# A one-core hybrid mixer with two attention layers: memory weights rounded on another engine, and E's gate, the dilated attention and even q rearranged

## The chip, the core and the metric

The kernel runs on one core of one Trainium2 chip. The metric is the device time of one execution in microseconds; three runs of the kernel before are given. TensorE (PE; its weight loads are PEld), VectorE (DVE), ScalarE (ACT) and GpSimd (POOL) each run their own program in order; SyncE (SP) issues the weight loads.

## The reference

x is 1024 tokens by 1024 channels, the memory 256 tokens by 1024. A first block has five branches of width 512, each gated and merged; a second block has an even layer (dilated attention, pool, memory attention) and an odd layer.

```python
# first block
h = rms_norm(x);  ys = [y_a, y_b, y_c, y_d, eo * silu(e_z)]     # y_e: attention to k, v of the memory
merged = sum(sigmoid(gates[n]) * (ys[n] @ w_br[n]) for n in range(5))
x = x + rms_norm(merged @ w_out)
# even layer
qk, v_a, x_b, q_m, z = split(rmsnorm(x) @ w_in)
a_out = dilated_attention_mixer(qk, v_a, cos, sin)   # 4 heads; groups (128, 1), (512, 4), (2048, 16)
b_out = multiscale_pool(x_b, w_pool, scale)          # mean over 2, 4, 8, 16 tokens minus x_b, then w_pool
m_out = memory_attention(q_m, mem_n, w_mem_kv)
x = x + (concatenate([a_out, b_out, m_out]) * silu(z)) @ w_out
```

In dilated attention each group yields a numerator, a row maximum and a denominator; the three groups of a head are joined by exp(m_g - max m).

## The kernel before

**Dense products.** Channels lie on the partitions. Every dense product is made as three products of rounded parts (h_hi·w_hi, h_lo·w_hi, h_hi·w_lo; y_hi and y_lo for gated inputs). SP loads a weight tile of 8 (or 4) x 128x128 into one of two slots of w_raw; POOL makes w_hi from it (L3065, four instructions of 128x256) and w_lo (L3070, four), and counts `tiles_split`; TensorE multiplies with 512 tokens at a time (`dense_half`, L344), two PSUM halves in turn. The halves are taken by ScalarE (`project`, L399 and L401; `project_away`, L1237, which sends them to DRAM in L1214; `memory_kv`, L1340), or by VectorE (`merge`, L474 and L476, behind ScalarE's sigmoid L458; `add_out`, L492).

**Order.** `section()` opens a part of the program with three threads, dense, aux and side. `stage(name, us, ahead, ...)` adds to a thread a piece for some of PE, ACT and DVE, with a planned length; each engine's program merges the threads by planned time (`play`, L3010), and runs in that order. Before its part in a stage, an engine waits for what the other engines have done in the stages ahead in the thread, unless it stands in `ahead` (`thread_part`, L2995).

**Memory keys and values.** E's k (`memory_beside`, beside D's x), E's v, and k and v of the even and the odd layer (`memory_kv`) are 24 weight tiles for 256 columns each. Even and odd k v run beside branch A's chunk work (L1622, L1713, L1741 to L1756) and branch B's convolution on VectorE (taps L1532).

**E.** E's attention (L2035, L2051, L1010, L1020) runs beside D's merge; then the E gate (`gate_stored`: per half tile L1285 product with z, L1287 y_hi, L1288 y_lo, all VectorE) and E merge, with the angle work of rope (L2112 to L2133) on VectorE in another thread. Stage "C merged" is a `drain` on TensorE that waits for VectorE's parts ahead of it.

**Dilated attention** (`dilated_attention`, L2376). A head has 18 slots: 6 turn v (L2426), 12 are pairs of blocks. For a pair in slot i: scores on TensorE (L2437, L2438) at i, bias, maximum (L2518, L2525, L2526, VectorE) at i + 0.4, exponentials (L2486, ScalarE) at i + 1, turn (L2447, TensorE) at i + 1.4, copy (L2495, ScalarE) at i + 1.8, mix (L2460, TensorE) at i + 2.2, take (L2532 to L2537, VectorE) at i + 2.5. Buffers of pairs alternate: bias of pair m waits for the turn of pair m - 2. The stages of the next head's projections (L344) fill the time between, with rope (L2352 to L2355) on VectorE. `dilated_join` (L2562 spread on TensorE, L2585 and L2596 ScalarE, L2589 to L2628 VectorE) joins a head. Beside head 3 runs "pool x"; behind it "even q", then the pool sums (L2701 to L2706), "x back", "even out A" (`add_out`, waits for join 3) and pool mix (L2735). The output x is kept in DRAM (`x_fm`) meanwhile.

## Time and profile before

| | us |
|---|---|
| three runs | 3713.05, 3718.22, 3718.74 (median 3718.22) |
| the profiled execution, its span | 3720.16, 3718.3 |
| TensorE busy, its weight loads | 3428.0 (92%), 2787.2 (75%) |
| VectorE busy | 1769.0 (48%) |
| GpSimd busy | 1568.3 (42%) |
| ScalarE busy | 907.8 (24%) |

Busy shares are averages over stages with different limits: TensorE at 92% still idles 290 us, and those are spread over many waits. The mean clock granted to TensorE is 0.966 of full speed; the stretches below 1 lie mostly at waits.

### The profile page before, as it was taken

What the parts mean: (1) busy time and instruction counts of PE and PEld (TensorE: products, weight loads), DVE (VectorE), ACT (ScalarE), POOL (GpSimd) and SP (SyncE); (2) the same over time, 40 slices, a digit from 0 to 9 for tenths busy, and PEclk for the clock granted to TensorE, in tenths of its full rate; (3) what the DMA queues carried; (4) which work ended last, traced back from release to release, by engine and by line L of the source; (5) the groups of instructions that cost most, each with busy time, mean ns of one, the idle gap of its engine ahead of it and who ended that gap; (6) DMA issues with size and microseconds to landing.
All of it is one profiled execution on the core that took longest, in us unless ns stands there. A gap on an engine that the chain in (4) does not pass through costs nothing.

```text
span 3718.3 us, 44394 instructions
## 1 busy us (share of the span) xinstructions
PE 3428.0 (92%) x16512; PEld 2787.2 (75%) x16512; DVE 1769.0 (48%) x2634; ACT 907.8 (24%) x1780; POOL 1568.3 (42%) x2013
## 2 busy tenths in 40 slices
PE   7989989999999999899899899889969989999988
PEld 6778888886786677677677587778757767788767
DVE  4733688774124454533523546675552444412343
ACT  3222212223014432333012322222221122310021
POOL 3454582233452245534444254353314334424423
PEclk9999999999999999999999999999979999999999
DMA  3122121111131021231112111010102101211211
GB/s 116 46 71 60 45 87 26 46 49 47 56 96 41 26 66 34 63 102 40 50 48 91 66 46 29 29 35 22 30 17 88 51 24 46 63 46 37 80 37 68
DMA packets 297208, 196.98 MB, mean 53 GB/s; under 512 B 25365, under 2 KB 277273, under 8 KB 297017
## 3 DMA queue, kind: packets, MB, share of 16 engines
q1 hardware_dynamic: 271241, 132.77, 13.0%
q10 hardware_dynamic: 25776, 61.56, 4.5%
q8 instruction: 132, 2.16, 0.3%
q14 instruction: 59, 0.48, 0.0%
HBM read 168.87 MB, written 25.44 MB: 52 GB/s over the span
## 4 chain that ended last, share of the span: by engine, by line
PE 62%; DVE 11%; PEld 3%; ACT 3%; issue 2%; POOL 2%; DMA 1%; ACTq 0%; PEldq 0%; DVEq 0%; POOLq 0%
PE ps L344 49%; PE ps L982 2%; PEld ps L344 2%; PE ps L1622 2%; POOL w_lo L3070 1%; PEld ps L2562 1%; PE ps L2051 1%; PE ps L995 1%; ACT wrk L1010 1%; POOL w_hi L3065 1%; PE ps L2460 1%; PE ps L1915 1%; PE ps L2447 1%; PE ps L2438 1%; DVE wrk L2604 1%
## 5 line engine op out<-in xcount | busy, mean ns | idle before, releaser
L3065 POOL TENSOR_TENSOR w_hi<-w_raw,pool_one 128x256 fp32r<-128x256 f32 x1004 | 682.0, 708 | 2097.7 <-PE ps L344 2060.6
L344 PE MATMUL ps<-h_hi,w_hi 128*128 128x512 f32 x2928 | 1212.3, 414 | 94.9 <-POOL w_lo L3070 28.2
L344 PE MATMUL ps<-h_hi,w_lo 128*128 128x512 f32 x2928 | 1158.1, 396 | 0.0
L344 PE MATMUL ps<-h_lo,w_hi 128*128 128x512 f32 x2928 | 1157.3, 395 | 0.0
L3070 POOL TENSOR_TENSOR w_lo<-w_raw,w_hi 128x256 fp32r<-128x256 f32 x1004 | 887.3, 913 | 23.1
L344 PEld LDWEIGHTS ps<-h_hi,w_hi 128*128 128x128 f32 x2928 | 560.7, 192 | 265.9 <-issue 104.2
L344 PEld LDWEIGHTS ps<-h_hi,w_lo 128*128 128x128 f32 x2928 | 559.0, 191 | 123.1
L344 PEld LDWEIGHTS ps<-h_lo,w_hi 128*128 128x128 f32 x2928 | 561.9, 192 | 107.6 <-issue 5.5
L344 PE MATMUL ps<-y_hi,w_hi 128*128 128x512 f32 x704 | 287.7, 409 | 15.8 <-issue 11.9
L344 PE MATMUL ps<-y_hi,w_lo 128*128 128x512 f32 x704 | 276.0, 392 | 0.0
L344 PE MATMUL ps<-y_lo,w_hi 128*128 128x512 f32 x704 | 276.0, 392 | 0.0
L1532 DVE SCALAR_TENSOR_TENSOR y_spare<-y_spare_hi,cols,y_spare 128x511 f32<-128x511 f32 (+28 forms) x232 | 200.3, 905 | 2.2 <-DVE y_spare L1532 0.5
L1622 PE MATMUL ps<-wrk 128*128 128x128 f32 x1216 | 162.4, 282 | 18.9 <-DVE wrk L1741 5.0
L474 DVE TENSOR_TENSOR wrk<-ps,wrk 128x512 f32<-128x512 f32 x64 | 44.2, 691 | 279.9 <-PE ps L344 278.8
L1622 PEld LDWEIGHTS ps<-wrk 128*128 128x128 f32 x1216 | 154.7, 196 | 29.5 <-POOL w_lo L3070 10.7
L344 PEld LDWEIGHTS ps<-y_hi,w_hi 128*128 128x128 f32 x704 | 133.3, 189 | 55.9 <-issue 25.5
L458 ACT ACTIVATE wrk<-ps,cols 128x512 f32<-128x512 f32 x80 | 55.2, 689 | 430.6 <-PE ps L344 401.9
L344 PEld LDWEIGHTS ps<-y_lo,w_hi 128*128 128x128 f32 x704 | 133.2, 189 | 29.7 <-issue 3.6
L344 PEld LDWEIGHTS ps<-y_hi,w_lo 128*128 128x128 f32 x704 | 133.1, 189 | 28.6
L492 DVE TENSOR_TENSOR acc<-acc,ps 128x512 f32<-128x512 f32 x72 | 49.5, 687 | 151.3 <-PE ps L344 150.2
L436 DVE TENSOR_TENSOR wrk<-wrk 128x512 f32<-128x512 f32 x48 | 38.5, 803 | 158.1 <-ACT wrk L425 157.9
L1713 ACT ACTIVATE wrk<-ps 128x256 f32<-128x256 f32 x112 | 42.6, 385 | 211.7 <-PE ps L1622 199.1
(399 smaller groups left out, 3950.7 us busy)
## 6 DMA issues: line engine op xcount, KB each, us to landing
w_raw<-in_w_in SPq DMA_DIRECT2D x87, 512.0 KB
w_raw<-in_even_w_in SPq DMA_DIRECT2D x48, 512.0 KB
away<-wrk ACTq DMA_DIRECT2D x64, 256.0 KB, 2.1
w_raw<-in_odd_w_in SPq DMA_DIRECT2D x32, 512.0 KB
wrk<-away ACTq DMA_DIRECT2D x24, 512.0 KB
wrk<-in_x ACTq DMA_DIRECT2D x16, 512.0 KB, 8.0
w_raw<-in_w_br SPq DMA_DIRECT2D x32, 256.0 KB
w_raw<-in_even_w_out SPq DMA_DIRECT2D x24, 256.0 KB
```

The source lines that it names most:

```text
L344: mm = nc.tensor.matmul(ps[:, b, 0:n], w[:, slot, k, :], rhs(part, k, b), start=(k == 0 and q == 0), stop=(k == nk - 1 and q == 2))
L436: ch.link(nc.vector.tensor_tensor(o(j, b), o(j, b), wt(sz, b), ALU.mult))
L458: nc.scalar.activation(wt(gt, b), ps[:, b, :], ACT.Sigmoid, bias=gate_bias(i)).then_inc(dense_free[b], 1)
L474: nc.vector.tensor_tensor(wt(gt, b), ps[:, b, :], wt(gt, b), ALU.mult).then_inc(dense_free[b], 1)
L492: nc.vector.tensor_tensor(y, x, ps[:, b, :], ALU.add).then_inc(dense_free[b], 1)
L982: mm = nc.tensor.matmul(S[:, u, c], l, r, start=True, stop=True)
L995: mm = nc.tensor.transpose(PT[:, kb, u, :], SB[:, u, lo + kb * P:lo + (kb + 1) * P], ident)
L1532: ins = nc.vector.scalar_tensor_tensor(y, x, b_tap(s, i), y, ALU.mult, ALU.add)
L1622: mm = nc.tensor.matmul(four(dst)[:, h, :], lhsT(h), rhs(h), start=True, stop=True)
L1713: nc.scalar.activation(ZZ[:, two, :], four(2 + p)[:, two, :], ACT.Copy).then_inc(gdn_act.sem, 1)
L3065: ins = nc.gpsimd.tensor_tensor(hi, raw, one[:, 0:2], ALU.mult)
L3070: ins = nc.gpsimd.tensor_tensor(lo, raw, hi.bitcast(F32), ALU.subtract)
```

## The change

Five parts. (A) `round_tile`: for the 24 memory tiles ScalarE makes w_hi in one instruction of 128x1024, behind an eviction of its own; POOL then only makes w_lo and waits on `hi_by_act`. (B) Stage "C merged" has TensorE in `ahead`. (C) `gate_stored` for E is replaced by `gate_products` (the products with z, a stage behind E's attention, in the section before) and `gate_parts` (y_hi by ScalarE, y_lo by VectorE). (D) Turn, copy, mix and take of a pair come at i + 2.0, 2.4, 3.0 and 3.4, and a head is planned at 22.0 slots instead of 21.2. (E) Even q goes to DRAM beside head 3 and comes back into acc 4 to 7 after the pool sums; pool x follows it, into acc 4 to 7; even out A stands beside the pool sums in the same section; the lower half of x is loaded behind pool x, the upper one behind join 3.

```diff
         def f_dve(dve):
-            if sum_there:
-                sum_there(dve)
             for j in range(r.n):
                 for b in range(2):
                     yield when(r, j, b)
+                    if sum_there and b == 0:
+                        sum_there(dve, j)
                     out_ready(dve, r.t0 + j, b)
                     x, y = (old or acc_at)(j, b), (new or acc_at)(j, b)
                     nc.vector.tensor_tensor(y, x, ps[:, b, :], ALU.add).then_inc(dense_free[b], 1)
...
+    def gate_products(name, o, z_first, us=8.0):
+
+        gated = sig.take("y_gated", 8)
+
+        def f_dve(dve):
+            for b in range(2):
+                ngates[b] += 1
+                for j in range(4):
+                    yield (4 * b + j) / 8
+                    if j == 0:
+                        dve.wait_ge(gate_loaded[b], 16 * ngates[b])
+                    nc.vector.tensor_tensor(o(j, b), o(j, b), gate_tiles(z_first[b])[:, j, :],
+                                            ALU.mult).then_inc(gated.sem, 1)
+        stage(name, us, dve=f_dve)
+        return gated
+
+    def gate_parts(name, o, gated, before, us=8.0):
+
+        rounded = sig.take("y_rounded", 8)
+        done = sig.take("y_done", 8)
+        part = lambda t, j, b: t[:, j, b * HALF:(b + 1) * HALF]
+
+        def f_act(act):
+            out_ready(act, before.t0 + before.n - 1, 1)
+            for i in range(8):
+                yield i / 9
+                act.wait_ge(gated.sem, gated.nth(i))
+                nc.scalar.activation(part(y_hi, i % 4, i // 4), o(i % 4, i // 4), ACT.Copy).then_inc(rounded.sem, 1)
+
+        def f_dve(dve):
+            out_ready(dve, before.t0 + before.n - 1, 1)
+            for i in range(8):
+                yield (i + 0.9) / 9
+                dve.wait_ge(rounded.sem, rounded.nth(i))
+                nc.vector.tensor_tensor(part(y_lo, i % 4, i // 4), o(i % 4, i // 4),
+                                        part(y_hi, i % 4, i // 4).bitcast(F32), ALU.subtract).then_inc(done.sem, 1)
+        stage(name, us, ("act", "dve"), act=f_act, dve=f_dve)
+        return done
+
...
+    project("A project", r_a, a_tile, lambda j: col("b_aqkv", j), after=lambda act, j: round_tile(act, r_a.t0 + j + 2))
...
-    def memory_kv(name, w_kv, which, kind, place, after_wide):
+    def round_tile(act, t):
+        if t in act_tiles:
+            act.wait_ge(raw_loaded[t % 2], 32 * (t // 2) + 32)
+            act.wait_ge(dense_out, 2 * t - 2)
+            nc.scalar.activation(w_hi[:, t % 2], w_raw[:, t % 2], ACT.Copy).then_inc(hi_by_act, 1)
+
...
+    stage("C merged", 0.1, ("pe",), pe=c_merged_pe)
     on("aux")
...
-    def e_there(dve):
-        dve.wait_ge(e_attended.sem, e_attended.nth(0))
-    stage("E attention there", 0.1, dve=e_there)
-    e_done = gate_stored("E gate", wt, (6, 8))
+    e_done = gate_parts("E gate in parts", wt, e_gated, r_dm)
...
-                events.append((i + 1.4, i, lambda m=m, g=g: turn(m, g)))
-                events.append((i + 2.2, i, lambda m=m, g=g, n=n: mix(m, g, n)))
+                events.append((i + 2.0, i, lambda m=m, g=g: turn(m, g)))
+                events.append((i + 3.0, i, lambda m=m, g=g, n=n: mix(m, g, n)))
             yield from in_time(events)
+            if h == 3:
+                pe.drain().then_inc(last_mixed.sem, 1)
...
-                events.append((i + 1.8, i, lambda m=m, g=g: copy(m, g)))
+                events.append((i + 2.4, i, lambda m=m, g=g: copy(m, g)))
...
-                events.append((i + 2.5, i, lambda m=m, g=g, n=n: take(m, g, n)))
+                events.append((i + 3.4, i, lambda m=m, g=g, n=n: take(m, g, n)))
...
+            at_eq2 = project_away("even q", run(2, *both(w2, C2_Q)), None, None, 1.2, lambda b: wt(9, b))
             r_px = run(2, *both(w2, C2_X))
-            project("pool x", r_px, acc_at, before=lambda act, j, b: head_free(act, 4))
+
+            def x_room(act, j, b):
+                head_free(act, 4)
+                if j == 3:
+                    act.wait_ge(last_mixed.sem, last_mixed.nth(0))
+            project("pool x", r_px, lambda j, b: acc_at(4 + j, b), before=x_room, pace=1.2)
+
+            def x_lower(act):
+                act.dma_start(acc[:, 0:4, :], x_fm.rearrange("k p t -> p k t")[:, 0:4, :]).then_inc(x_lower_in, 16)
+                stored_away(act)
+            stage("lower half of x back", 0.5, act=x_lower)
         on("aux")
         stage("head z before the groups", 11.0)
...
+
+    def first_sum(j, b):
+        return acc_at(j, b) if j < 4 else wt(j, b)
+
+    def x_there(dve, j):
+        dve.wait_ge(x_lower_in if j < 4 else x_upper_in, 16)
+    add_out("even out A", run(4, *both(w2o[0], 0), 4, 4), lambda pe, k, b: pe.wait_ge(join_done.sem, join_done.nth(3)),
+            x_there, first_sum, first_sum)
+    pool_summed = sig.take("pool_summed", 1)
+
+    def pool_sums_there(act):
+        act.wait_ge(pool_summed.sem, pool_summed.nth(0))
+    stage("pool sums there", 0.1, act=pool_sums_there)
     on("aux")
 
     def p_load(act):
+        act.wait_ge(join_done.sem, join_done.nth(3))
+        act.dma_start(wrk[:, 4:8, :], x_fm.rearrange("k p t -> p k t")[:, 4:8, :]).then_inc(x_upper_in, 16)
         load(act, wt(9)[:, 0:HALF].rearrange("p (g d) -> p g d", g=4),
              A["even_w_pool_2"][0].rearrange("g c d -> c g d"))
         yield 0.9
         loads_done(act)
-
-    def x_upper(act):
-        act.wait_ge(join_done.sem, join_done.nth(3))
-        load(act, wrk[:, 4:8, :], x_fm.rearrange("k p t -> p k t")[:, 4:8, :])
-    on("side")
-    stage("last head joined", 22.0)
-    stage("upper half of x back", 0.5, act=x_upper)
-    on("aux")
...
@@ -2704,26 +2784,13 @@
             ch.link(nc.vector.tensor_tensor(small[:, 64:80], src[:, 0:16], C("icount")[:, 16 * i:16 * i + 16], ALU.mult))
             ch.link(nc.vector.scalar_tensor_tensor(wt(i), src, 1.0 / s, x, ALU.mult, ALU.subtract))
             ch.link(nc.vector.tensor_tensor(wt(i)[:, 0:16], small[:, 64:80], x[:, 0:16], ALU.subtract))
-    stage("pool weights", 5.0, act=p_load)
+        dve.drain().then_inc(pool_summed.sem, 1)
+    stage("pool weights, upper half of x back", 5.0, act=p_load)
     stage("pool sums", 26.0, dve=p_dve)
 
...
+    def q_back(act):
+        act.dma_start(acc[:, 4:8, :], away[at_eq2:at_eq2 + 4].rearrange("j p t -> p j t")).then_inc(even_q_in, 16)
+    stage("even q back", 0.5, act=q_back)
...
+
+    def even_q_there(pe):
+        pe.wait_ge(even_q_in, 16)
+    stage("even q there", 0.1, pe=even_q_there)
...
-        def split(t, s, raw_count, nk):
+        def split(t, s, raw_count, nk, by_pool, rounded):
             pool.wait_ge(raw_loaded[s], raw_count)
-            for k in range(0, nk, 2):
+            if rounded is not None:
+                pool.wait_ge(hi_by_act, rounded)
+            for k in range(0, nk, 2) if rounded is None else ():
                 raw, hi, lo = w_raw[:, s, k:k + 2], w_hi[:, s, k:k + 2], w_lo[:, s, k:k + 2]
                 ins = nc.gpsimd.tensor_tensor(hi, raw, one[:, 0:2], ALU.mult)
-            ins.then_inc(hi_ready, 1)
-            pool.wait_ge(hi_ready, t + 2)
+            if rounded is None:
+                ins.then_inc(hi_ready, 1)
+                pool.wait_ge(hi_ready, by_pool)
```

Where the E gate runs, VectorE's queue before (wrk holds E's output and the stored z, ps the PSUM halves):

```order
L2056 COPY wrk<-ps 128x512
L474 TENSOR_TENSOR wrk<-ps,wrk 128x512
L476 TENSOR_TENSOR acc<-acc,wrk 128x512
...
L476 TENSOR_TENSOR acc<-acc,wrk 128x512
L1285 TENSOR_TENSOR wrk<-wrk 128x512
L1287 CAST y_hi<-wrk 128x512
L1288 TENSOR_TENSOR y_lo<-wrk,y_hi 128x512
...
L1288 TENSOR_TENSOR y_lo<-wrk,y_hi 128x512
L2112 CAST wrk<-wrk 32x1024
```

and of the change (L479, L481, L1310, L1333, L2171 are L474, L476, L1285, L1288, L2112 of before):

```order
L2117 COPY wrk<-ps 128x512
L1310 TENSOR_TENSOR wrk<-wrk 128x512 x8
L479 TENSOR_TENSOR wrk<-ps,wrk 128x512
L481 TENSOR_TENSOR acc<-acc,wrk 128x512
...
L481 TENSOR_TENSOR acc<-acc,wrk 128x512
L1333 TENSOR_TENSOR y_lo<-wrk,y_hi 128x512 x8
L479 TENSOR_TENSOR wrk<-ps,wrk 128x512
L481 TENSOR_TENSOR acc<-acc,wrk 128x512
...
L481 TENSOR_TENSOR acc<-acc,wrk 128x512
L2171 CAST wrk<-wrk 32x1024
```

The products with z stand ahead of D's last two gate tiles, y_hi has left the queue, and the first evictions of the E merge stand ahead of the angle work.

In even k v, ScalarE's queue before (L1713 evicts branch A's chunks, L1340 memory tiles):

```order
L1214 DMA away<-wrk 128x512 x2
L1713 ACTIVATE wrk<-ps 128x256 x2
L1340 ACTIVATE wrk<-ps 128x128 x2
L1713 ACTIVATE wrk<-ps 128x256 x2
L1340 ACTIVATE wrk<-ps 128x128 x2
L1713 ACTIVATE wrk<-ps 128x256 x2
L1340 ACTIVATE wrk<-ps 128x128 x2
```

and of the change (L1774, L1394 and L1219 are L1713, L1340 and L1214 of before):

```order
L1774 ACTIVATE wrk<-ps 128x256 x2
L1394 ACTIVATE wrk<-ps 128x128 x2
L1370 ACTIVATE w_hi<-w_raw 128x1024
L1219 DMA away<-wrk 128x512 x2
L1774 ACTIVATE wrk<-ps 128x256 x2
L1394 ACTIVATE wrk<-ps 128x128 x2
L1370 ACTIVATE w_hi<-w_raw 128x1024
L1774 ACTIVATE wrk<-ps 128x256 x2
```

A rounding of 128x1024 stands behind each memory tile's evictions.

From the end of head 3 to the pool mix, ScalarE's queue before (L2585 and L2596: join; L399: pool x, then even q; L1073: loads):

```order
L2495 ACTIVATE wrk<-ps 128x256
L2585 ACTIVATE wrk<-ps 128x1024
...
L2585 ACTIVATE wrk<-ps 128x16x64
L2596 ACTIVATE wrk<-wrk 128x1024 x3
L1073 DMA wrk<-in_even_w_pool 128x4x128
L399 ACTIVATE acc<-ps 128x512 x4
L1073 DMA wrk<-x_fm 128x4x1024
L399 ACTIVATE acc<-ps 128x512
L1073 DMA acc<-x_fm 128x4x1024
L399 ACTIVATE acc<-ps 128x512 x3
L2742 ACTIVATE wrk<-ps,cols 128x512 x8
```

and of the change (L1243 evicts even q, L402 pool x, L2646 and L2657 are the join, L2809 the pool mix):

```order
L1243 ACTIVATE wrk<-ps 128x512
L1219 DMA away<-wrk 128x512
...
L402 ACTIVATE acc<-ps 128x512 x2
L2646 ACTIVATE wrk<-ps 128x1024
...
L2646 ACTIVATE wrk<-ps 128x16x64
L402 ACTIVATE acc<-ps 128x512 x3
L2657 ACTIVATE wrk<-wrk 128x1024 x3
L402 ACTIVATE acc<-ps 128x512 x3
L2737 DMA acc<-x_fm 128x4x1024
L2766 DMA wrk<-x_fm 128x4x1024
L1078 DMA wrk<-in_even_w_pool 128x4x128
L2792 DMA acc<-away 128x4x1024
L2809 ACTIVATE wrk<-ps,cols 128x512 x7
```

Five of pool x's evictions stand ahead of the join's exponentials L2657 now, and nothing but loads stands between pool x and the pool mix.

## Rows read from the trace of the kernel before

**Rows 1.** page, part 1: busy us, share, instructions of each engine
```profile
PE 3428.0 (92%) x16512; PEld 2787.2 (75%) x16512; DVE 1769.0 (48%) x2634; ACT 907.8 (24%) x1780; POOL 1568.3 (42%) x2013
```

**Rows 2.** waits on TensorE: line <- what ended it: us in total, times, longest
```profile
PE ps L2447 <- ACT wrk L2486: 37.0, 14, 6.9
PE ps L344 <- POOL w_lo L3070: 28.2, 24, 4.0
PE ps L344 <- ACT acc L399: 19.3, 1, 19.3
```

**Rows 3.** windows, 434 to 548 us: busy us of each engine, clock, DMA
```profile
434.00:548.00 114.00, 92.30 (x708) 89.10 (x708) 105.29 (x145) 22.04 (x75) 105.98 (x118) 0.94 0.27 79
```

**Rows 4.** lines by form, 434 to 548 us; last: window of L1532
```profile
L3070 POOL TENSOR_TENSOR w_lo<-w_raw,w_hi 128x256 fp32r<-128x256 f32 x60 | 58.5, 1005 | 1.2
L3065 POOL TENSOR_TENSOR w_hi<-w_raw,pool_one 128x256 fp32r<-128x256 f32 x58 | 49.1, 875 | 6.8 <-PE ps L357 6.7
...
440.00:548.00 108.00, 64.33 (x61) 0.94 0.29 84
```

**Rows 5.** source: all instructions of L1532 and L1577, ns least/median/most
```profile
L1532 DVE SCALAR_TENSOR_TENSOR y_spare<-y_spare_hi,cols,y_spare x232: 700/748/1291, 440.8 to 835.4; 128x511 f32<-128x511 f32 x4, 128x510 f32<-128x510 f32 x4, 128x509 f32<-128x509 f32 x4, 128x508 f32<-128x508 f32 x4
L1577 ACT ACTIVATE acc<-wrk x8: 1038/1049/1063, 113.3 to 187.1; 128x1024 f32<-128x1024 f32 x8
```

**Rows 6.** timeline, 1571 to 1608 us: start, us, instruction [idle before]
```profile
1571.79 0.76 PE L344 MATMUL ps<-h_hi,w_hi 128*128 128x512 f32 x1 [6.16 <-DVEq L3008]
...
1595.10 2.75 ACTq L1073 DMA_DIRECT2D wrk<-away  x6
...
1607.38 1.97 PE L2035 MATMUL ps<-cst,wrk 128*128 128x128 f32 x8 [3.63 <-ACTq L3008]
```

**Rows 7.** timeline, VectorE, 1778 to 1818 us, at D merge and E gate
```profile
1778.30 0.69 DVE L474 TENSOR_TENSOR wrk<-ps,wrk 128x512 f32<-128x512 f32 x1 [13.31 <-PE ps L344]
1800.00 0.69 DVE L1285 TENSOR_TENSOR wrk<-wrk 128x512 f32<-128x512 f32 x1 [0.45 <-issue]
...
1817.19 1.09 DVE L1288 TENSOR_TENSOR y_lo<-wrk,y_hi 128x512 fp32r<-128x512 f32 x1
```

**Rows 8.** timeline, TensorE and ScalarE, 1818 to 1833 us, start of E merge
```profile
1818.80 0.69 ACT L458 ACTIVATE wrk<-ps,cols 128x512 f32<-128x512 f32 x1 [25.50 <-DVEq L3008]
...
1819.58 0.77 PE L344 MATMUL ps<-y_hi,w_hi 128*128 128x512 f32 x1 [9.91 <-issue]
...
1832.21 0.77 PE L344 MATMUL ps<-h_hi,w_hi 128*128 128x512 f32 x1 [4.51 <-DVE wrk L474]
```

**Rows 9.** windows, TensorE alone: 24 products after a wait, 90 at full clock
```profile
1819.58:1827.70 8.12, 8.12 (x24) 0.68 0.24 70
2840.00:2860.00 20.00, 20.00 (x90) 1.00 0.21 60
```

**Rows 10.** timeline, head 2: first turn, a later turn, a bias
```profile
2504.79 1.11 PE L2447 MATMUL ps<-cst,wrk 128*128 128x128 f32 x4 [6.87 <-ACT wrk L2486]
...
2561.51 0.44 PE L2447 MATMUL ps<-cst,wrk 128*128 128x128 f32 x2 [3.85 <-ACT wrk L2486]
...
2501.55 0.74 DVE L2518 SCALAR_TENSOR_TENSOR wrk<-ps,cst 128x256 f32<-128x256 f32 x2
```

**Rows 11.** timeline: head 3's join, pool sums, even out A's end
```profile
2740.39 8.44 PE L2562 MATMUL ps<-cst,small 128*128 128x128 f32 x48 [10.96 <-DVEq L3008]
...
2779.54 0.77 PE L344 MATMUL ps<-h_hi,w_hi 128*128 128x512 f32 x1 [19.31 <-ACT acc L399]
...
2774.44 1.23 DVE L2628 TENSOR_TENSOR y_lo<-wrk,y_hi 128x1024 fp32r<-128x1024 f32 x1
2791.73 0.15 DVE L2701 COPY wrk<-acc 128x1 f32<-128x1 f32 x1
2799.72 0.59 DVE L2706 TENSOR_TENSOR wrk<-small,acc 128x16 f32<-128x16 f32 x1
...
2866.28 0.47 PE L344 MATMUL ps<-h_hi,w_hi 128*128 128x512 f32 x1 [0.26 <-POOL w_lo L3070]
```

67 lines of the change are left out of this document (40 added, 27 removed).

## The prediction

> **What bounds the kernel now.** I read the page first: TensorE is busy 3428 of 3718.3 us [rows 1], so everything that can be won is in its 290 us of idle time and in the stretches at the lower clock. The view of waits on TensorE then says what ends its idle time: 37.0 us in dilated attention, where the turn L2447 waits for the exponentials, 28.2 us for rounded weights, one wait of 19.3 us for a ScalarE eviction [rows 2]. The timeline adds 10.96 us of spread L2562 behind the join on VectorE [rows 11] and 6.16 us for a stage on VectorE [rows 6]. Four of these five are what the change touches, and each is read in its own stretch below. About 0.2% (7.4 us) is what a measurement of this kernel can tell from no change. The sum is made against the profiled execution (3720.2 us, span 3718.3); the median of the runs shown is 2 us lower.
>
> **A. ScalarE rounds 24 weight tiles (memory k, v).** Removed from POOL: 24 x 4 L3065. Added: 24 ScalarE instructions of 128x1024 and a wait of POOL on them. Nearest row for the price: L1577, the same size, 1049 ns [rows 5]. Eight tiles lie in E k and E v, whose gaps I found to wait for the wide tile that POOL still rounds, or for VectorE: 0. Sixteen lie in 434 to 548 us. There POOL works 106.0 of 114 us, VectorE 105.3, TensorE 92.3 and ScalarE 22.0 [rows 3]: POOL and VectorE share the bound. POOL loses the 49.1 us of L3065 and stops bounding; ScalarE gains 16 x 1.05 = 17 us, hidden in its 92 idle us. VectorE bounds next. Its 61 taps cost 64.3 us there [rows 4], 1055 ns each, against a median of 748 ns over the kernel [rows 5]: 61 x 0.31 = 19 us of slowing beside POOL, and some 4 us on other two-operand instructions. L3065 is 49.1 of POOL's 107.6 us [rows 4], so 46% of that goes: 10.5 us. VectorE then needs 95 us, TensorE some 90. I take **-12**; ends: -3 (VectorE's order does not let it use the time) and -18 (down to TensorE's own time).
> The Trainium skill (SBUF — State Buffer, Who interferes with whom) calls the port pair of VectorE and GpSimd an exclusive lock for a whole instruction. The trace agrees that taps slow down beside POOL (1055 against 748 ns), not that they alternate wholly: taps, roundings and subtractions side by side would not fit 114 us. By the rule all of L3065's time would leave the shared port, and the term would be at its end of -18.
>
> **B. "C merged" no longer waits for VectorE.** TensorE's gap of 6.16 us at 1565.6 goes. But the next wait, 3.63 us at 1603.8 [rows 6], is for a load that ScalarE issues at 1595.10, behind VectorE's D gate, and that anchor does not move: it grows by what the first loses. **0** (-2 to +2).
>
> **C. E gate.** The 24 VectorE instructions (L1285, L1287, L1288 for 8 half tiles) start at 1800.00 and end at 1818.3 [rows 7]; ScalarE's sigmoid waits until then, and TensorE, which has only one gate tile meanwhile, idles 9.91 us and then 4.51 us, since the first eviction L474 stands behind nine angle instructions [rows 8]. Then 24 products take 8.12 us at clock 0.68 [rows 9]; at full clock 90 take 20.00 us, so 24 would take 5.3: 2.8 us lost, and as much again behind the second wait (that row's clock was 0.84). After the change the 8 products L1285 run in VectorE's idle 13.31 us before 1778.3 [rows 7], where 8 x 0.69 = 5.5 us fit. ScalarE rounds, at the 0.69 us of its 128x512 sigmoids [rows 8], while VectorE subtracts, at 0.69 us as L1285 or up to 1.09 beside POOL [rows 7], one behind the other: from 1799.6 the pair ends between 1806 and 1809, before TensorE finishes its gate tile at 1809.7. The first two evictions now stand ahead of the angles. Gone: 9.9 + 4.5 + 2.8 + 2.9 = 20; left: perhaps 1 us of handing over. **-19** (-14 to -21). What ScalarE is asked for, it has time for: it idles there.
>
> **D. Attention lags.** Per head, TensorE's turn moves from 1.4 to 2.0 slots after its scores, mix from 2.2 to 3.0. The waits inside the groups (0.7, 3.9 and 1.7 us in heads 0 to 2; 3.85 us is the row at 2561.51 [rows 10]) are 18.6 us with 3 us of lower clock, and mostly go. The first wait of a head does not: 6.87 us at 2504.79 and its like [rows 10] stand behind VectorE's chain of join and rope, which has no hole; in three places they lose nothing and gain about 1.4 us. 3.85 us behind rope goes to 2 to 3. Longer attention puts 6 more products ahead of each head's last mix: nothing by itself, they are work moved. **-8** (-15 to -2).
>
> **E. Even q beside head 3, out A beside the sums.** Before, after the last mix (2721.2) TensorE waits 10.96 us, then 19.31 us for ScalarE's eviction [rows 11], which sits behind a load that waits for join 3; the join ends at 2775.7, and even out A with pool mix ends at 2866.3: 145 us from the last mix. Even q's 192 products and pool x's 192 are the same number after, only earlier. After, from the last mix: 18 products 4.2 us, spread and 18 products 10.0, 72 products 16.6 (ScalarE's exponentials stand behind these evictions), the second spread and 18 products 10.0, and VectorE's part of the join as before, from the end of the spread, 2748.8, to 2775.7, or 26.8: the join ends 67.6 us after the mix. TensorE has but 42 products (9.7 us) left meanwhile, so it waits some 17 us for the join, half of the 30.3 that go. Out A: 192 products at 0.222 to 0.231 [rows 9], 44; pool mix with its waits, as before, 7; evictions behind pool sums, since VectorE's queue now holds sums between them: the sums take some 21 us in four parts, the last one 2791.7 to 2800.3 or 8.6 [rows 11], while two PSUM halves give 5.5 us: 4.5 to 8; lower clock after the wait 2 to 3. Together 126 to 130, so -15 to -19; attention with 24 more products in head 3 (5.5 us, less 3.5 of its waits) gives back 2, and the sends of even q (room for two halves on ScalarE's queue, which in other places land in 2 us) nothing. **-13** (-20 to -5).
>
> Sum: -12 + 0 - 19 - 8 - 13 = -52. The profiled execution would take 3668 us, the median of the runs shown 3666; I say **3667 us**.
>
> **The rivals.**
> 1. *The gains of D and E come back as waits* (chance 0.2). For: each wait that goes in a chain bound by VectorE makes TensorE arrive earlier at the next. Against: inside the groups VectorE has idle time. D 0, E -3, A -8, C -19: -30, **3688**.
> 2. *The clock comes back too* (0.2). Fewer gaps mean fewer stretches at the lower clock; the mean is 0.94 in A's stretch. A -18, C -21, D -15, E -18: -72, **3646**.
> 3. *VectorE holds the memory stretch alone* (0.1). It is in order and 92% busy there: A gives -2, the rest as forecast: -42, **3676**.
> 4. *Slower: the turns close a loop* (0.06). VectorE's bias of pair m waits for TensorE's turn of pair m-2, since both use one buffer. Its margin falls from 1.0 to 0.4 slots, with bias, maximum, exponentials and turn behind it. A, C and E give -44; from a wait of (44 + 7.4) / 48 = 1.1 us for each of the 48 pairs the kernel is slower; at 1.5 us it is +72 - 44 = +28, **3746**. For: rope's long instructions stand in the same queue. Against: the bias of a pair takes 0.74 us [rows 10]; with the maximum and the exponentials at about as much each, and the hand-overs, the loop needs some 3 us (an estimate), and its two slots of TensorE's work last about 6.
> 5. *The change does not do what it says* (0.04): ScalarE's rounding starts only when the slot is free and comes behind evictions that wait for TensorE, so POOL waits for it as long as it worked before, and E's products find their z not loaded: A and C give -6, D and E -8: -14, **3704**.
>
> **How the numbers follow.** The forecast has 0.40. Its bounds run from -70 to -32; with rivals 1 to 3 the range is **3644 to 3698**, leaving out rivals 4, most of 5 and the tail. Faster by over 0.2%: 0.90; within 0.2%: 0.04; slower: 0.06.
>
> **What would show it.** In the profile after: TensorE's waits for ACT L399 and for the stage at 1571 gone; at the E merge no idle over 2 us; POOL in 434 to 536 at two thirds of its time, and the taps there near 0.95 us; the wait at L2035 (now another line) 8 to 10 us; PE's first turn in each head still waiting 4 to 8 us, later turns hardly at all; one wait of 15 to 20 us for join 3 ahead of out A, and some us in its evictions. I am wrong in D if the waits for exponentials sum to over 30 us; in E if the join ends later than 75 us after the last mix; in A if the stretch takes over 110 us.

## The result, and the profile after

The changed kernel takes 3671.64 us (median of 4 runs, 3669.43 to 3672.26) against 3717.68 us (4 runs of the kernel before, three of them those shown above): the ratio is 0.9876, with a 95% interval of 0.986 to 0.9891, or 46 us less (41 to 52). The profiled execution spans 3667.4 us, 50.9 us less than that of before. The forecast was 3667 us.

The first part of the page:

```profile
PE 3410.8 (93%) x16512; PEld 2769.2 (76%) x16512; DVE 1766.4 (48%) x2626; ACT 934.1 (25%) x1812; POOL 1508.4 (41%) x1917
```

TensorE's busy time fell from 3428.0 [rows 1] to 3410.8 us although it does the same 16512 products: that is the clock, whose mean went from 0.966 to 0.972. The other 34 us of the 50.9 are idle time. The view of waits on TensorE (L347, L2506 and L1243 are L344, L2447 and L1237 of before):

```profile
PE ps L347 <- POOL w_lo L3144: 28.3, 25, 4.0
...
PE ps L2506 <- ACT wrk L2547: 16.8, 6, 8.4
PE ps L347 <- DVEq L2690: 15.9, 1, 15.9
...
PE ps L347 <- ACT wrk L1243: 8.8, 3, 5.6
...
PE ps L347 <- DVE acc L497: 7.1, 3, 3.4
PE ps L347 <- ACT wrk L402: 6.8, 1, 6.8
PE ps L347 <- ACT acc L402: 6.8, 1, 6.8
...
PE ps L347 <- DVE wrk L497: 4.4, 1, 4.4
```

Against [rows 2], the 37.0 us behind exponentials are 16.8, and the 19.3 us behind L399 are gone. New are 15.9 us behind the join, two waits of 6.8 us behind evictions L402, and 11.5 us behind evictions L497 of even out A; the waits behind L1243 grew from 2.2 to 8.8 us. The dense products' 28.3 us of waiting for weights are what they were: part A shortens such waits at other lines (see A).

Since the products are the same in number and order over long stretches, the two traces can be laid side by side at the same instruction, and each part be read alone. The times are those of the start of a wait, and for E attention's first product and the first turns those of the instruction behind it; "shift" is after minus before:

| place | before | after | shift |
|---|---|---|---|
| first wait in the stretch of even k v | 433.9 | 434.1 | +0.2 |
| 743.7 before, branch A's next chunk | 743.7 | 727.2 | -16.5 |
| ahead of "C merged" | 1484.9 | 1469.5 | -15.4 |
| E attention's first product | 1607.4 | 1593.8 | -13.6 |
| behind the E merge | 1957.7 | 1923.5 | -34.2 |
| first turn of head 1 | 2355.9 | 2322.0 | -33.8 |
| first turn of head 2 | 2504.8 | 2468.7 | -36.1 |
| first turn of head 3 | 2653.8 | 2613.6 | -40.2 |
| end of the last mix | 2721.2 | 2681.3 | -39.9 |
| even memory attention | 2927.2 | 2879.2 | -48.1 |
| end | 3718.3 | 3667.4 | -50.9 |

So A gave 16.7 us, B took 1.8, C gave 20.6 to 21.5 (-13.6 at E attention, -12.7 when it ends, -34.2 behind the merge), D 5.7, E 8.2. Two differences belong to no part: 1.0 us lost at 1447.7 us, where the first product behind the same wait of 2.83 us took 0.79 us instead of 0.50 and those behind it were slower too, and 3 us won at the end, behind all edits.

**A.** Windows of the changed kernel: length, busy us of PE, PEld, DVE, ACT and POOL, TensorE's clock.

```profile
434.00:532.00 98.00, 87.76 (x709) 84.88 (x708) 90.37 (x140) 33.36 (x86) 60.43 (x64) 0.97 0.31 92
1797.00:1833.00 36.00, 34.61 (x151) 27.85 (x150) 27.49 (x29) 3.43 (x5) 21.89 (x26) 1.00 0.16 44
2747.34:2820.00 72.66, 61.06 (x221) 45.81 (x222) 34.24 (x48) 4.55 (x7) 32.12 (x40) 0.90 0.30 98
```

The window of 114 us [rows 3] ended behind the wait that closes the stretch, this one of 98 us ends ahead of it; from the start of the first wait to the end of the last the stretch took 114.2 us and takes 99.0. POOL is busy 60.4 us of it, as against 106.0. Lines by form in that stretch, and last the window of the taps (L1593 is L1532):

```profile
L3144 POOL TENSOR_TENSOR w_lo<-w_raw,w_hi 128x256 fp32r<-128x256 f32 x60 | 58.2, 1000 | 42.8 <-ACT w_hi L1370 42.8
...
L1370 ACT ACTIVATE w_hi<-w_raw 128x1024 fp32r<-128x1024 f32 x14 | 15.2, 1087 | 0.0
...
434.00:532.00 98.00, 54.02 (x58) 0.97 0.31 92
```

POOL's subtractions take 1000 ns as before [rows 4]; what it gained is 42.8 us in which it waits for ScalarE's rounding, 1087 ns each. The taps went from 1055 to 54.02 / 58 = 931 ns. TensorE's waits of 0.5 us and more in the stretch were 13.5 us for rounded weights, 5.0 for VectorE and 2.4 for an eviction; now they are 5.6, 3.1 and none.

**B.** Timeline of TensorE, then of ScalarE, from 1582 us:

```profile
1586.16 0.79 PE L347 MATMUL ps<-h_hi,w_hi 128*128 128x512 f32 x1 [5.58 <-ACT wrk L1243]
...
1593.79 1.94 PE L2096 MATMUL ps<-cst,wrk 128*128 128x128 f32 x8 [2.64 <-ACTq L3079]
```

```profile
1582.53 2.79 ACTq L1078 DMA_DIRECT2D wrk<-away  x6
1585.42 0.69 ACT L1243 ACTIVATE wrk<-ps,cols 128x512 f32<-128x512 f32 x1 [14.07 <-issue]
```

The 6.16 us [rows 6] are gone, and the wait at L2096 (L2035) did not take them. An eviction of E's z, L1243, did: it stands in ScalarE's queue behind the six loads of L1078, and those wait for VectorE's D gate, whose last instruction ends at 1582.4. TensorE, early now, waits 5.58 us for it, at the lower clock afterwards (0.79 for its first product), and then 2.64 us for the loads.

**C.** Timeline of VectorE (L1310 products with z, L1333 y_lo) and of ScalarE:

```profile
1753.34 2.50 DVE L1310 TENSOR_TENSOR wrk<-wrk 128x512 f32<-128x512 f32 x4 [1.05 <-ACTq L3079]
...
1787.03 6.12 DVE L1333 TENSOR_TENSOR y_lo<-wrk,y_hi 128x512 fp32r<-128x512 f32 x8 [0.21 <-ACT y_hi L1326]
1799.80 0.69 DVE L479 TENSOR_TENSOR wrk<-ps,wrk 128x512 f32<-128x512 f32 x1 [6.66 <-PE ps L347]
```

```profile
1793.28 0.69 ACT L463 ACTIVATE wrk<-ps,cols 128x512 f32<-128x512 f32 x1 [3.67 <-DVEq L3079]
...
1796.98 0.69 ACT L463 ACTIVATE wrk<-ps,cols 128x512 f32<-128x512 f32 x1 [3.02 <-PE ps L347]
```

The products ran in VectorE's idle time beside D merge. The eight L1333 take 6.12 us in one piece from 1787.0 to 1793.2, and the sigmoid starts at 1793.28. The first eviction L479, at 1799.80, stands ahead of the angles. The waits of 9.91 and 4.51 us [rows 8] are gone: the window 1797 to 1833 has TensorE busy 34.6 of 36 us, at clock 1.00.

**D.** Timeline of TensorE and ScalarE at the start of head 2's attention:

```profile
2444.11 0.47 PE L347 MATMUL ps<-h_hi,w_hi 128*128 128x512 f32 x1 [1.79 <-ACT y_spare L2714]
...
2464.82 0.77 PE L347 MATMUL ps<-h_hi,w_hi 128*128 128x512 f32 x1 [6.80 <-ACT wrk L402]
...
2468.69 0.66 PE L2506 MATMUL ps<-cst,wrk 128*128 128x128 f32 x4 [0.97 <-ACT wrk L2547]
```

```profile
2464.08 0.60 ACT L402 ACTIVATE wrk<-ps 128x512 f32<-128x512 f32 x1 [14.08 <-DVEq L2690]
```

Before, TensorE came to the first turn with a wait of 6.87 us [rows 10] and then turned. Now it stops earlier, behind an eviction L402 that waits for the join (ScalarE idle 14.08 us), has 2.9 us of products to make after that (six, at the lower clock), and then waits 0.97 us more for the turn's exponentials. These waits look new, but they hang on the same chain. The last instruction of head 1's join on VectorE, before and then after:

```profile
2498.14 1.56 DVE L2628 TENSOR_TENSOR y_lo<-wrk,y_hi 128x1024 fp32r<-128x1024 f32 x1
```

```profile
2462.50 1.52 DVE L2689 TENSOR_TENSOR y_lo<-wrk,y_hi 128x1024 fp32r<-128x1024 f32 x1
```

The first turn comes 5.1 us behind the join's end before and 4.7 us after (4.5 and 4.7 in head 1, 4.3 and 4.6 in head 3), so the eviction adds nothing. What grew is the time to the join's end. Each head begins with TensorE's products of its z, beside the join of the head before it, and with a short wait for ScalarE's eviction of z (L2714); all times "from z" here count from the start of that wait. From z of heads 1, 2 and 3 to the end of that join it was 17.3, 17.6 and 17.8 us and is 21.7, 21.7 and 21.1. The join needs the old head's last mix, and the lag moved that mix nearer to z: 174 dense products lie between the two instead of 186, 52.5 us instead of 55.3. The rest is the way from that mix to the join's end, 73.7 to 74.3 us instead of 72.6 to 73.0; why that way grew is open.

**E.** Timeline of TensorE and of VectorE from the join's end (L2689) on:

```profile
2747.34 0.76 PE L347 MATMUL ps<-y_hi,w_hi 128*128 128x512 f32 x1 [15.85 <-DVEq L2690]
...
2760.89 0.53 PE L347 MATMUL ps<-y_hi,w_hi 128*128 128x512 f32 x1 [3.40 <-DVE acc L497]
...
2794.77 0.50 PE L347 MATMUL ps<-y_hi,w_hi 128*128 128x512 f32 x1 [4.37 <-DVE wrk L497]
```

```profile
2745.94 1.23 DVE L2689 TENSOR_TENSOR y_lo<-wrk,y_hi 128x1024 fp32r<-128x1024 f32 x1
...
2785.36 0.15 DVE L2781 COPY wrk<-acc 128x1 f32<-128x1 f32 x1
...
2794.03 1.29 DVE L497 TENSOR_TENSOR wrk<-wrk,ps 128x512 f32<-128x512 f32 x2 [0.23 <-DVE wrk L2786]
```

The join ends 65.9 us after the last mix. The wait for it is 15.85 us. Then out A waits 3.40, 1.85, 1.87 and 4.37 us for L497, each time behind a whole group of sums: the group of 8.6 us (2785.36 to 2794.0) ends just before the eviction at 2794.03. The first group is short, 3.9 us, but it had itself waited 3.34 us for ScalarE's load of the pool weights. The window 2747.34 to 2820 has clock 0.90: 7 us of its 72.7. Windows of TensorE behind the wait for the join and behind the first three of the four waits (length, busy us, clock):

```profile
2747.34:2757.00 9.66, 9.66 (x35) 0.81 0.68 244
2760.89:2770.90 10.01, 10.01 (x36) 0.83 0.02 6
2772.78:2778.40 5.62, 5.62 (x24) 1.00 0.16 47
2780.34:2790.00 9.66, 9.66 (x35) 0.82 0.09 27
```

So of the 7 us some 1.8 stand behind the wait for the join, and some 5 behind the evictions; the wait of 1.85 us was followed by none, that of 1.87 us by 1.7.

### The profile page after: what moved, and what is told of

Same layout as the page of the kernel before. It is cut to its first block, busy times and chain, and to the rows that moved or that the text cites. A ratio compares the mean times of both kernels' runs of the same rounds, so it can differ in the third digit from the quotient of the medians.

```text
span 3667.4 us, 44376 instructions
## 1 busy us (share of the span) xinstructions
PE 3410.8 (93%) x16512; PEld 2769.2 (76%) x16512; DVE 1766.4 (48%) x2626; ACT 934.1 (25%) x1812; POOL 1508.4 (41%) x1917
## 4 chain that ended last, share of the span: by engine, by line
PE 59%; DVE 10%; PEld 6%; issue 3%; ACT 3%; POOL 2%; DMA 1%; PEldq 0%; ACTq 0%; DVEq 0%; POOLq 0%
PE ps L347 47%; PEld ps L347 4%; PE ps L987 2%; PE ps L1683 2%; POOL w_lo L3144 2%; PEld ps L2623 1%; PE ps L1000 1%; PE ps L2112 1%; POOL w_hi L3138 1%; ACT wrk L1015 1%; PE ps L1976 1%; PE ps L2519 1%; DVE wrk L2665 1%; DVE wrk L680 0%; PEld ps L2519 0%
## 5 line engine op out<-in xcount | busy, mean ns | idle before, releaser
L3138 POOL TENSOR_TENSOR w_hi<-w_raw,pool_one 128x256 fp32r<-128x256 f32 x908 | 615.3, 706 | 1987.9 <-PE ps L347 1965.6
L347 PE MATMUL ps<-h_hi,w_hi 128*128 128x512 f32 x2928 | 1208.6, 413 | 85.8 <-POOL w_lo L3144 28.3
L347 PE MATMUL ps<-h_hi,w_lo 128*128 128x512 f32 x2928 | 1154.9, 394 | 0.0
L347 PE MATMUL ps<-h_lo,w_hi 128*128 128x512 f32 x2928 | 1154.3, 394 | 0.0
L347 PEld LDWEIGHTS ps<-h_hi,w_hi 128*128 128x128 f32 x2928 | 558.9, 191 | 259.3 <-issue 90.9
L347 PEld LDWEIGHTS ps<-h_hi,w_lo 128*128 128x128 f32 x2928 | 557.0, 190 | 121.8
L347 PEld LDWEIGHTS ps<-h_lo,w_hi 128*128 128x128 f32 x2928 | 559.7, 191 | 108.3 <-issue 6.0
L347 PE MATMUL ps<-y_hi,w_hi 128*128 128x512 f32 x704 | 289.6, 411 | 32.8 <-DVEq L2690 15.9
L347 PE MATMUL ps<-y_lo,w_hi 128*128 128x512 f32 x704 | 278.5, 396 | 0.0
L347 PE MATMUL ps<-y_hi,w_lo 128*128 128x512 f32 x704 | 278.5, 396 | 0.0
L1593 DVE SCALAR_TENSOR_TENSOR y_spare<-y_spare_hi,cols,y_spare 128x511 f32<-128x511 f32 (+28 forms) x232 | 193.6, 877 | 2.2 <-DVE y_spare L1593 0.5
L347 PEld LDWEIGHTS ps<-y_hi,w_hi 128*128 128x128 f32 x704 | 134.6, 191 | 73.7 <-issue 34.1
L479 DVE TENSOR_TENSOR wrk<-ps,wrk 128x512 f32<-128x512 f32 x64 | 44.2, 691 | 268.7 <-PE ps L347 267.7
L347 PEld LDWEIGHTS ps<-y_lo,w_hi 128*128 128x128 f32 x704 | 134.7, 191 | 30.0 <-issue 3.1
L347 PEld LDWEIGHTS ps<-y_hi,w_lo 128*128 128x128 f32 x704 | 134.7, 191 | 29.2
L497 DVE TENSOR_TENSOR acc<-acc,ps 128x512 f32<-128x512 f32 x72 | 49.2, 687 | 121.4 <-PE ps L347 120.1
L1774 ACT ACTIVATE wrk<-ps 128x256 f32<-128x256 f32 x112 | 42.4, 384 | 184.9 <-PE ps L1683 176.0
```

What stands on the lines that cost most here:

```text
L347: mm = nc.tensor.matmul(ps[:, b, 0:n], w[:, slot, k, :], rhs(part, k, b), start=(k == 0 and q == 0), stop=(k == nk - 1 and q == 2))
L479: nc.vector.tensor_tensor(wt(gt, b), ps[:, b, :], wt(gt, b), ALU.mult).then_inc(dense_free[b], 1)
L497: nc.vector.tensor_tensor(y, x, ps[:, b, :], ALU.add).then_inc(dense_free[b], 1)
L1593: ins = nc.vector.scalar_tensor_tensor(y, x, b_tap(s, i), y, ALU.mult, ALU.add)
L1774: nc.scalar.activation(ZZ[:, two, :], four(2 + p)[:, two, :], ACT.Copy).then_inc(gdn_act.sem, 1)
L3138: ins = nc.gpsimd.tensor_tensor(hi, raw, one[:, 0:2], ALU.mult)
```

## The experiments

Each group of kernels has its own runs of the kernel before beside it (3717.7 us for the change, then 3721.5, 3720.2 and 3723.5 us). Ratios are therefore compared, not times.

### Each part alone

**only_A**: the code of `round_tile` and what belongs to it, on the kernel before.

```diff
+    def round_tile(act, t):
...
+            nc.scalar.activation(w_hi[:, t % 2], w_raw[:, t % 2], ACT.Copy).then_inc(hi_by_act, 1)
...
+            if rounded is not None:
+                pool.wait_ge(hi_by_act, rounded)
```

> Part A alone on the kernel before: ScalarE rounds the 24 memory tiles. Theory: the stretch of even and odd k v was held by POOL and VectorE together, the two slowing each other; comparing the two traces by their landmarks gives 16 to 17 us there and nothing at the eight tiles of E: 3700 to 3703 us, the stretch at 97 to 99 instead of 114 us. Rival: VectorE's order holds it alone once POOL is free and part of the gain in the changed kernel came from elsewhere: 3708 to 3716.

Measured: ratio 0.9959 (0.9944 to 0.9974), 15 us less (10 to 21). The median, 3706.5 us, lies between the two expectations; the stretch decides. From the start of the wait at 430.8 to the start of the one at 528.7 it takes 98 us (112.4 before, counted in the same way), as the theory says.

**only_B**:

```diff
-    stage("C merged", 0.1, pe=c_merged_pe)
+    stage("C merged", 0.1, ("pe",), pe=c_merged_pe)
```

> Part B alone: stage C merged does not wait for VectorE. Theory: the wait of 6.2 us only moves, to evictions that stand behind the load for E's attention and to that load itself, and a second gap at the lower clock makes it 1 to 3 us dearer: 3718 to 3721 us. Rival: the loss of 3 us between the landmarks of the two traces is not B's; then the gap is won or moved without loss: 3712 to 3718.

Measured: ratio 1.0001 (0.9992 to 1.001). TensorE's timeline:

```profile
1606.17 0.80 PE L344 MATMUL ps<-h_hi,w_hi 128*128 128x512 f32 x1 [5.56 <-ACT wrk L1237]
...
1614.07 1.97 PE L2035 MATMUL ps<-cst,wrk 128*128 128x128 f32 x8 [3.02 <-ACTq L3008]
```

The wait moved as in the changed kernel, to the same eviction. From the wait for weights at 1485 us of before (1488 here) to E attention's first product it takes 126.2 us instead of 122.5, 3.7 us more. The times exclude neither 0 nor 3 us.

**only_C**:

```diff
-    e_done = gate_stored("E gate", wt, (6, 8))
+    e_gated = gate_products("E gated", wt, (6, 8))
...
+    e_done = gate_parts("E gate in parts", wt, e_gated, r_dm)
```

> Part C alone: products of E with z beside D's merge, y_hi by ScalarE, y_lo by VectorE. Theory: both gaps at the start of the E merge (9.9 and 4.5 us) shrink to 1 us together, and with the clock 20 to 22 us are won: 3696 to 3698 us. Rival: ScalarE and VectorE hand over too slowly unless B has brought the load forward: a gap of 3 to 5 us stays, 3701 to 3706.

Measured: ratio 0.9938 (0.9923 to 0.9953), 23 us less (17 to 29). No wait over 0.5 us is left at the start of the E merge (0.48 us at 1812.01 is the longest), without B: the rival falls, and C needs nothing of B.

**only_D**:

```diff
-                events.append((i + 1.4, i, lambda m=m, g=g: turn(m, g)))
-                events.append((i + 2.2, i, lambda m=m, g=g, n=n: mix(m, g, n)))
+                events.append((i + 2.0, i, lambda m=m, g=g: turn(m, g)))
+                events.append((i + 3.0, i, lambda m=m, g=g, n=n: mix(m, g, n)))
```

> Part D alone: the lag of turn, copy, mix and take. Theory: per head the waits inside the groups go (some 7 us with the clock) and 3 to 4 us come back as a longer wait before the head's first turn and an eviction that stands behind the join; with three heads this is 5 to 7 us in all: 3711 to 3713 us. Rival: the lag stands in head 3 without the projections of even q beside it and has nothing to fill with there, so that the last mix comes later: 0 to 3 us won, 3715 to 3718.

Measured: ratio 0.9986 (0.9976 to 0.9995), 5 us less (2 to 9). It is between the two, and the times alone do not decide. The trace has the same waits as the changed kernel in heads 1 and 2:

```profile
2503.40 0.77 PE L344 MATMUL ps<-h_hi,w_hi 128*128 128x512 f32 x1 [6.80 <-ACT wrk L399]
...
2507.54 1.12 PE L2447 MATMUL ps<-cst,wrk 128*128 128x128 f32 x4 [1.25 <-ACT wrk L2486]
```

From 2073 us (2067.5 before) to the end of the last mix it takes 647.4 us instead of 653.6: 6.2 us won, nearly what the changed kernel shows (5.7). The join of heads 0 to 2 ends 21.7 to 22.0 us behind the wait for z here too.

**only_E**: even q beside head 3 with the old lag, out A beside the sums.

> Part E alone on the kernel before (even q beside head 3 with the old lag, out A beside the pool sums). Theory: what E takes from the waits of 11.0 and 19.3 us it gives back as 16 us of waiting for join 3, 11 us in out A's evictions behind the sums, and the lower clock behind each: 5 to 9 us are left, 3710 to 3714 us. Rival: without the lag, head 3 has no products to spare for its waits, E gains under 3 us: 3716 to 3720; or E is worth 15 us by itself and loses it only beside D: 3703 to 3706.

Measured: ratio 0.9991 (0.9982 to 1.0001), 3 us less (7 less to none). TensorE's timeline in head 3 and out A:

```profile
2652.04 1.12 PE L2448 MATMUL ps<-cst,wrk 128*128 128x128 f32 x4 [7.39 <-ACT wrk L2489]
...
2785.94 0.77 PE L344 MATMUL ps<-y_hi,w_hi 128*128 128x512 f32 x1 [14.52 <-DVEq L2632]
...
2830.49 0.79 PE L344 MATMUL ps<-y_hi,w_hi 128*128 128x512 f32 x1 [4.64 <-DVE wrk L492]
```

The pattern is the changed kernel's: 14.5 us for the join and 4.6 us in the last of four waits for evictions. Head 3's first turn waits 7.39 us instead of 4.61 without any lag; whether E causes that is open, since the same wait in heads 1 and 2, whose code E leaves alone, was 6.27 and 4.45 us here and 4.40 and 6.87 us before. The trace and the times do not agree on E's size. In the profiled execution, the fastest of the ten, it takes 286.0 us from the wait for head 3's z to the even memory attention instead of 295.5: 9.5 us, near the 8.2 of the changed kernel and in the theory's 5 to 9; the ten times give 3. Either way E is not a gain of 15 us that D spoils.

The five measured differences add up to 15 + 0 + 23 + 5 + 3 = 46 us, what the whole change gives. Each is uncertain by 3 to 6 us, so this shows no dependence of the parts on each other, and excludes only a large one.

### B undone in the changed kernel

**no_B**:

```diff
-    stage("C merged", 0.1, ("pe",), pe=c_merged_pe)
+    stage("C merged", 0.1, pe=c_merged_pe)
```

> The changed kernel with part B undone. Theory: B alone changed nothing on the kernel before, and beside the other parts it moves the same wait: within 3 us of the changed kernel (3670 to 3675). Rival: the 3 us lost between 1445 and 1594 us of the changed kernel's trace are B's: 3667 to 3670.

Measured: ratio 0.9866 (0.9846 to 0.9886) where the whole change has 0.9876 (0.986 to 0.9891). The times leave both open. The wait of 6.16 us is back, and the one for the loads is longer than in the kernel before:

```profile
1594.55 1.97 PE L2096 MATMUL ps<-cst,wrk 128*128 128x128 f32 x8 [4.16 <-ACTq L3079]
```

From the wait for weights at 1470.3 us to this product it takes 124.3 us, and as much in the changed kernel: here the trace shows no price of B.

### What E gave back

**fine_sums**: the same sums, with more places where an eviction can come between.

```diff
...
             for lv in range(i + 1):
+                if lv:
+                    yield done / 14
+                done += 1
...
+            yield done / 14
+            done += 1
             ch.link(nc.vector.tensor_tensor(small[:, 64:80], src[:, 0:16], C("icount")[:, 16 * i:16 * i + 16], ALU.mult))
```

> The changed kernel with VectorE's pool sums cut into 14 pieces where evictions of even out A can come between, instead of 4. Theory: the four waits of TensorE in out A (3.4, 1.9, 1.9, 4.4 us) are evictions queued behind a whole group of sums, and the lower clock in 2748 to 2820 us follows them: 8 to 16 us are won, 3656 to 3664. Rival: out A waits because VectorE as a whole is late there (it begins the sums at 2756, and pool mix then waits for the sums): the waits move to pool mix, 3668 to 3673.

Measured: ratio 0.9845 (0.9828 to 0.9862), 0.0031 under the changed kernel's 0.9876, or 11 to 12 us. TensorE's timeline in out A, and the window of out A with the pool mix:

```profile
2762.64 0.50 PE L347 MATMUL ps<-y_hi,w_hi 128*128 128x512 f32 x1 [1.33 <-DVE acc L497]
...
2771.71 0.47 PE L347 MATMUL ps<-y_hi,w_hi 128*128 128x512 f32 x1 [0.61 <-DVE acc L497]
...
2778.02 0.47 PE L347 MATMUL ps<-y_hi,w_hi 128*128 128x512 f32 x1 [0.59 <-DVE acc L497]
```

```profile
2751.00:2813.00 62.00, 58.20 (x226) 43.13 (x226) 34.29 (x49) 6.11 (x8) 33.24 (x40) 0.97 0.36 116
```

The waits of 11.5 us became 2.8, and the clock in the window is 0.97 instead of 0.90: behind the join's wait of 15.85 us it is 0.83 over 10.8 us as before, and behind the waits that are left it is 1.00 (2762.64 to 2800). From the z of head 3 to the even memory attention it takes 278.7 us instead of 291.3. Pool mix then waits 0.7 us for the sums: the rival is out. In this kernel the evictions' order was worth 8.7 us of waits and, as the rest of the 12.6 us, about 4 us of clock.

**fine_sums_early**:

```diff
-    stage("pool sums", 26.0, dve=p_dve)
+    stage("pool sums", 26.0, ("dve",), dve=p_dve)
```

> As the kernel with the sums in 14 pieces, and the sums do not wait for ScalarE's load of the pool weights either, so that they can start at the join's end instead of 8.5 us later. Theory: if the evictions behind the sums were the cost, this adds 0 to 2 us of gain over the fine pieces alone. Rival (VectorE as a whole is late): most of the gain comes only here, 4 to 10 us more than with the pieces alone.

Measured: ratio 0.9848 (0.9831 to 0.9864): nothing more, though only one wait for an eviction of 0.5 us or more is left in out A (0.76 us). VectorE as a whole was not late.

### How many of the tiles count, and what holds the stretch after A

**A16**: part A without the 8 tiles of E's k and v.

```diff
-    memory_kv("E v", weights("w_mem_kv"), 0, 1, at_kv[0] + 1, True, True)
+    memory_kv("E v", weights("w_mem_kv"), 0, 1, at_kv[0] + 1, True)
...
-        r.rounded = len(act_tiles)
-        r.both_rounded = False
-        act_tiles.extend(r.t(i, 0) for i in range(r.pairs))
```

> Part A alone, but only for the 16 tiles of even and odd k v; the 8 tiles of E's k and v stay with POOL. Theory: the gaps at E's tiles wait for the wide tile beside them, so these eight are worth nothing: within 2 us of part A alone (ratio to the kernel before 0.995 to 0.997). Rival: they carry 2 to 5 us of part A's 15: ratio 0.9965 to 0.998.

Measured: ratio 0.9945 (0.9929 to 0.996), not above part A alone (0.9959). The gaps at E's tiles are 4.00, 2.54 and 2.54 us with either, as in the kernel before. The eight gain nothing that can be seen.

**A_thin_taps**: part A, without the odd taps of the convolution's first half. The kernel leaves these taps out and so computes another convolution; it serves as a probe of VectorE's time.

```diff
         for s in taps:
+            if first == 0 and s % 2:
+                continue
```

> Part A alone, and the odd taps of the first half of branch B's convolution are left out (60 of VectorE's instructions, so the convolution is another one). Theory: after part A the stretch at 434 us is held by VectorE (90 us busy of 98); with 60 us less of it, TensorE's own 86 to 88 us hold it: the stretch falls to 88 to 92 us and the time is 6 to 10 us under part A alone, 3696 to 3701. Rival: TensorE and the hand-overs hold it already: the stretch stays at 96 to 98 us, 3704 to 3707.

Measured: ratio 0.994 (0.9924 to 0.9955), 7 us under part A alone and 2 us under A16, whose intervals overlap it. The stretch decides. The window 434 to 532 us of this kernel, and then of part A alone:

```profile
434.00:532.00 98.00, 90.53 (x734) 87.91 (x735) 64.35 (x108) 32.20 (x85) 57.41 (x69) 0.97 0.34 101
```

```profile
434.00:532.00 98.00, 90.00 (x723) 86.83 (x724) 90.55 (x137) 32.44 (x85) 61.32 (x65) 0.97 0.32 94
```

VectorE works 26 us less in the same 98 us, and TensorE is as busy as before, at 90 us. From the start of the wait at 431 us to the end of the one at 527 it takes 97.1 us, in part A alone 98.9. So my theory for this run fell, and the rival holds: after part A it is TensorE with its hand-overs that holds the stretch, not VectorE. Behind the stretch, up to 720 us, VectorE does still cost something: 3.2 us more are won there, and part A's two waits for it (1.26 us at 558, 0.60 us at 628) are gone.

### The size of the lag

**fine_sums_half_lag**:

```diff
-                events.append((i + 2.0, i, lambda m=m, g=g: turn(m, g)))
-                events.append((i + 3.0, i, lambda m=m, g=g, n=n: mix(m, g, n)))
+                events.append((i + 1.7, i, lambda m=m, g=g: turn(m, g)))
+                events.append((i + 2.6, i, lambda m=m, g=g, n=n: mix(m, g, n)))
...
-                events.append((i + 3.4, i, lambda m=m, g=g, n=n: take(m, g, n)))
+                events.append((i + 2.95, i, lambda m=m, g=g, n=n: take(m, g, n)))
```

> The changed kernel with the sums in 14 pieces and half of part D's lag (turn 1.7, copy 2.1, mix 2.6, take 2.95, 21.6 slots). Theory: the lag's gain lies in the turns that stand behind exponentials late by 1.7 to 3.9 us; a slot is some 3 us, so half the lag (1 us) leaves most of them: 3 to 6 us slower than with the full lag, 3665 to 3669. Rival: half the lag gives the same, since the chain of join and rope on VectorE sets each head's period: 3661 to 3664.

Measured: 3651.96 us, ratio 0.9807 (0.9792 to 0.9823), 0.0038 under fine_sums, or 14 us. Both sides of the expectation fell: half the lag is better than the whole. The same place as shown under D, on TensorE and, the end of the join, on VectorE:

```profile
2444.66 0.47 PE L347 MATMUL ps<-h_hi,w_hi 128*128 128x512 f32 x1 [3.12 <-ACT y_spare L2714]
...
2461.16 0.47 PE L347 MATMUL ps<-h_hi,w_hi 128*128 128x512 f32 x1 [2.58 <-ACT wrk L402]
...
2464.88 0.66 PE L2506 MATMUL ps<-cst,wrk 128*128 128x128 f32 x4 [2.09 <-ACT wrk L2547]
```

```profile
2458.79 1.57 DVE L2689 TENSOR_TENSOR y_lo<-wrk,y_hi 128x1024 fp32r<-128x1024 f32 x1
```

Inside a head it is as good as the full lag: from head 2's first turn to head 3's z it takes 119.7 us, with the full lag (fine_sums) 119.3, with the old one 127.0. Before the head it is better: from z to head 2's first turn 23.3 us, with the full lag 26.4, before 22.7. The join makes the difference. 180 dense products stand between the last mix and z, half way between 186 and 174; the mix is 53.9 us ahead of z, and the join ends 18.5, 18.8 and 18.6 us behind it, instead of 21.7, 21.7 and 21.1 with the full lag. The first turn follows 4.1 to 4.6 us later, much as before. TensorE's stop at the eviction L402, 2.58 us instead of 6.8, shows the same; the six products behind it take 1.6 us instead of 2.9, at full clock. Over heads 1 to 3 the way from z to the first turn is 9.3 us shorter than in fine_sums. The two profiled executions differ by 7.7 us in all, the ratios by 14.

**fine_sums_no_B**: fine sums, with part B undone.

> The changed kernel with the sums in 14 pieces and part B undone: the sum of the two edits that did not lose. Theory: B is worth 0 beside everything else, so this is within 3 us of the fine pieces with B: 3660 to 3665. Rival: the 3 us that the traces show at B are real: 3657 to 3660.

Measured: ratio 0.9838 (0.9821 to 0.9854) against 0.9845: the times do not tell. TensorE's timeline has the old pattern again:

```profile
1553.93 0.77 PE L347 MATMUL ps<-h_hi,w_hi 128*128 128x512 f32 x1 [6.16 <-DVEq L3085]
...
1588.70 1.97 PE L2096 MATMUL ps<-cst,wrk 128*128 128x128 f32 x8 [2.82 <-ACTq L3085]
```

From the wait for weights at 1467 us to E attention it takes 121.7 us; with B (fine_sums) 126.1. In the three pairs of traces that differ by B alone (before and only_B, these two, no_B and the change) B costs 3.7, 4.4 and 0.0 us at its place. That is a price of 0 to 4 us, and nothing won. In the times that is not settled: leaving it out gives -3.7 us (no_B), -2.6 us (here) and -0.4 us (only_B, turned round), each uncertain by more than 3.

The best version is the change with fine sums and half the lag: 3651.96 us, 71.8 us (66 to 77) less than the kernel before and some 26 us less than the change. Without B it was not tried.

## Why the prediction was right, and where its steps were off

The time, 3671.6 us, is 4.6 us from the forecast of 3667 and in the range 3644 to 3698. The sum held, and partly by luck: A and C gave more than forecast, B, D and E less, and the errors nearly cancelled. The terms, against what each part gave alone and between the landmarks:

| part | forecast | alone, by the ratio | landmarks |
|---|---|---|---|
| A | -12 (-18 to -3) | -15 (-21 to -10) | -16.7 |
| B | 0 (-2 to +2) | 0 (-3 to +4) | +1.8 |
| C | -19 (-21 to -14) | -23 (-29 to -17) | -20.6 to -21.5 |
| D | -8 (-15 to -2) | -5 (-9 to -2) | -5.7 |
| E | -13 (-20 to -5) | -3 (-7 to 0) | -8.2 (alone: -9.5) |

- **A, "VectorE bounds next".** This step was wrong in its mechanism. The stretch went to the end of -18 that the prediction called TensorE's own time. Of 16.7 us, the taps' faster pace gives 58 x 0.124 = 7 us of VectorE's time (I had 10.5 for taps and others), but thinning the taps by 26 us more moved the stretch by only 2: VectorE, 90 of 98 us busy, was hardly in TensorE's way there. The gain is mostly what POOL had held: TensorE's waits for rounded weights fell from 13.5 to 5.6 us. The eight tiles at 0 and ScalarE's rounding being hidden were right (1087 ns for the 1049 taken).
- **A and the shared port.** The rule of the Trainium skill (SBUF — State Buffer, Who interferes with whom) led to -18, nearer to the 16.7 found than my -12. That does not confirm a lock for a whole instruction: the gain ended at TensorE's time. Taps and POOL's work slow each other: the taps took 1055 ns beside both of POOL's instructions and 931 ns beside the subtractions alone, the subtractions 1000 ns, and 899 ns with the thinned taps. How the port is shared is not shown.
- **B.** That the wait only moves was right. Where to was wrong: I had looked at the load's consumer L2035 alone, and not at the evictions behind the same loads on ScalarE's queue.
- **C.** Right in each step, and the pair ended even sooner than said (6.3 us behind D merge's last sum, 6.4 to 9.4 forecast). The two gaps and the clock behind them were the 20 us worked out, and the hand-over costs next to nothing.
- **D, "lose nothing and gain about 1.4", and "work moved: nothing by itself".** This step was wrong. Inside the groups it went as forecast: from the E merge to head 1's z, and from the first turns of heads 1 and 2 to the next z, it takes 17.8 us less together (head 3, which also makes even q, takes 0.3 more). But from z to the first turn it takes 4.5, 3.7 and 3.7 us more, where the forecast had a gain of 1.4 in all. The prediction had the right chain, join and exponentials on VectorE and ScalarE, but took its place as fixed. It said that 6 more products come ahead of each head's last mix and cost nothing; there are 12, and they bring that mix, and with it the join, 2.7 us nearer to the next head's z. fine_sums_half_lag shows it: there it is 6 products and 1.4 us, and the join ends 18.5 to 18.8 us behind z instead of 21.1 to 21.7.
- **E, "evictions behind pool sums 4.5 to 8; lower clock 2 to 3".** The join came 65.9 us after the last mix (67.6 said), with a wait of 15.85 us (some 17 said). But the evictions cost 11.5 us, and the clock 7: some 1.8 behind the join, which was the term of 2 to 3, and some 5 behind three of the four waits for evictions, for which the sum had nothing. With 11.5 us for the evictions, 5 for the clock behind them and 1.7 off for the join, the 126 to 130 us become about 137, which is what is seen (145 less 8.2). fine_sums shows the step by taking it away.
- **The rivals.** Rival 1 had the mechanism that was seen: D and E give back at the chain of join and sums; but only half of it. Rival 4's loop (turn and bias) appears nowhere: whenever VectorE idles ahead of a bias, it is for the scores. Rival 5 does not appear either. Rival 2 was right on A and C alone.

## What to carry to other kernels

When work is put into one in-order queue beside evictions, its grain counts as much as its sum: groups of 5.8, 6.3 and 8.6 us, longer than the slack of two PSUM halves (24 products, 5.5 us here), stopped TensorE for 1.9, 1.9 and 4.4 us, though VectorE was busy only 30 of 39 us there. A lag that hides a wait inside a loop also moves the loop's last step nearer to what follows it; where a chain hangs on that last step, try half of the lag before all of it. And when a wait is said to move, go through every instruction behind the same anchor on each queue, not only the one that waits there now.

## What the runs showed of the hardware

Short waits can be dearer than they look: in even out A, waits of 3.40, 1.87 and 4.37 us were followed by stretches at a mean granted clock of 0.83, 0.82 and 0.93 (over 10, 10 and 25 us), some 5 us beside their 9.6; one of 1.85 us was followed by 1.00, and so were the waits of 0.6 us and the one of 1.33 us in fine_sums. A ScalarE rounding of 128x1024 takes 1087 ns. GpSimd's subtractions of 128x256 take 1005 ns with its own roundings between them and 1000 ns without, and 899 ns when VectorE makes fewer taps. Whether ScalarE's rounding slows GpSimd is not shown: in 434 to 532 us the two ran together for only 1 of the subtractions' 59 us.
